# The last expert taken out of the loops of a mixture-of-experts stage, with the next stage's first tiles split meanwhile and the row-pair sums made on VectorE

## What is computed

```python
def moe_ffn(h, router_w, router_b, w_gate_up, b_gate_up, w_down, b_down):
    logits = xt @ router_w + router_b
    top_v, top_i = lax.top_k(logits, TOP_K)            # TOP_K = 4
    gates = jax.nn.softmax(top_v, axis=-1)
    # for every expert e, over the tokens that chose it:
    gu = xb @ w_gate_up[e] + b_gate_up[e]
    act = x_glu * jax.nn.sigmoid(1.702 * x_glu) * (x_lin + 1.0)   # x_glu, x_lin clipped at 7
    out = act @ w_down[e] + b_down[e]                  # times its gate, added to the token's row
x = x + gate2 * rms_norm(moe_ffn(...), g_post_ffn)     # first block ends
x = layer_norm(ALPHA * x + 0.5 * (silu(x @ w1) * (x @ w3)) @ w2, g, b)   # second begins: f1
```

## Time and profile before

| | |
|---|---|
| median of 3 runs | 2604.8 us (2599.99, 2604.8, 2607.95) |
| span of the profiled execution | 2602.5 us |
| TensorE busy | 2430.7 us (93%) |
| VectorE, ScalarE, GpSimd busy | 1115.6, 824.6, 146.0 us |
| granted TensorE clock, mean of the span | 0.99 |
| experts | about 250 to 1233 us of the span |
| f1's first product | 1256.03 us |

### The profile page before, as it was taken

One profiled execution on the slowest core, in us unless ns is written; L12 is line 12 of the kernel. 1 busy time (PEld: TensorE's weight loads), 2 busy tenths in 40 slices (PEclk: granted clock), 3 DMA queues, 4 the chain that ended last, 5 costly groups with the idle time before them and its releaser, 6 DMA issues.

```text
span 2602.5 us, 31931 instructions
## 1 busy us (share of the span) xinstructions
PE 2430.7 (93%) x10874; PEld 1503.4 (58%) x10874; DVE 1115.6 (43%) x1605; ACT 824.6 (32%) x1227; POOL 146.0 (6%) x210
## 2 busy tenths in 40 slices
PE   8999999999988888888999998999999999999999
PEld 4756333333322222222688776777887887777787
DVE  4566111010111111111555677756556556876554
ACT  2322211111111111111444345343444444345443
POOL 0001100010100010000000000000000000100000
PEclk9999999999999999999999999999999999999999
DMA  8768999999999999998556552445555555434554
GB/s 311 270 211 312 411 420 419 421 405 413 406 421 421 421 416 411 407 411 354 174 185 205 168 165 97 162 146 170 186 187 173 188 185 194 150 105 162 170 185 146
DMA packets 263342, 700.36 MB, mean 269 GB/s; under 512 B 29379, under 2 KB 128107, under 8 KB 213536
## 3 DMA queue, kind: packets, MB, share of 16 engines
q1 hardware_dynamic: 249780, 685.19, 71.1%
q0 software_dynamic: 9360, 8.37, 1.0%
q10 hardware_dynamic: 4124, 5.77, 0.6%
HBM read 706.05 MB, written 23.63 MB: 280 GB/s over the span
## 4 chain that ended last, share of the span: by engine, by line
PE 41%; DVE 6%; ACT 2%; issue 2%; DMA 1%; POOL 0%; SPq 0%; POOLq 0%; DVEq 0%; ACTq 0%
PE bank L709 10%; PE bank L711 9%; PE bank L710 9%; PE bank L1313 3%; PE bank L1312 3%; PE bank L1311 3%; PE bank L859 1%; PE bank L801 1%; DVE w_lo L1456 1%; PE bank L1301 1%; PE bank L883 1%; PE bank L783 1%; DVE X L1712 0%; POOL st_out L2826 0%; DVE HTl L1507 0%
## 5 line engine op out<-in xcount | busy, mean ns | idle before, releaser
L1456 DVE TENSOR_TENSOR w_lo<-raw,w_hi 128x1024 fp32r<-128x1024 f32 (+3 forms) x405 | 488.7, 1216 | 342.4 <-ACT w_hi L2464 338.2
L2464 ACT ACTIVATE w_hi<-raw 128x1024 fp32r<-128x1024 f32 (+3 forms) x405 | 426.1, 1057 | 480.3 <-PE bank L711 281.1
L709 PE MATMUL bank<-w_hi,HTh 128*128 128x512 f32 (+1 forms) x1288 | 513.3, 399 | 13.2 <-DVE HTl L1507 8.0
L711 PE MATMUL bank<-w_hi,HTl 128*128 128x512 f32 (+1 forms) x1288 | 503.1, 391 | 0.0
L710 PE MATMUL bank<-w_lo,HTh 128*128 128x512 f32 (+1 forms) x1288 | 502.9, 390 | 0.0
L709 PEld LDWEIGHTS bank<-w_hi,HTh 128*128 128x128 f32 x1288 | 244.3, 190 | 66.5 <-DVE HTl L1507 12.5
L1159 PE MATMUL bank<-W_F,HT_F 128*64 128x512 f32 (+1 forms) x512 | 248.8, 603 | 34.9 <-DMA W_F<-in_moe_w 34.9
L2144 DVE TENSOR_SCALAR arena<-bank 64x512 f32<-64x512 f32 (+1 forms) x64 | 44.3, 693 | 548.9 <-PE bank L1160 548.9
L711 PEld LDWEIGHTS bank<-w_hi,HTl 128*128 128x128 f32 x1288 | 244.3, 190 | 51.9
L710 PEld LDWEIGHTS bank<-w_lo,HTh 128*128 128x128 f32 x1288 | 244.9, 190 | 46.7
L1160 PE MATMUL bank<-W_F,HT_F 128*64 128x512 f32 (+1 forms) x512 | 248.9, 603 | 0.0
(11 more groups left out here) (439 smaller groups left out, 3401.8 us busy)
## 6 DMA issues: line engine op xcount, KB each, us to landing
W_F<-in_moe_w SPq DMA_DIRECT2D x128, 1024.0 KB, 27.2
raw<-in_moe_w SPq DMA_DIRECT2D x64, 1024.0 KB
arena<-in_moe_w SPq DMA_DIRECT2D x64, 1024.0 KB, 26.9
raw<-in_ffn_w SPq DMA_DIRECT2D x248, 256.0 KB, 2.9
raw<-in_ffn_w_gu SPq DMA_DIRECT2D x164, 256.0 KB, 3.0
raw<-in_w_in SPq DMA_DIRECT2D x76, 512.0 KB, 4.8
MIX<-in_moe_w SPq DMA_DIRECT2D x32, 1024.0 KB, 25.1
HT_F<-in_moe_w SPq DMA_DIRECT2D x32, 1024.0 KB
```

Of the source, the lines that this page charges most:

```text
L709: pe.matmul(acc, xh, wh, start=start, stop=False)
L711: return pe.matmul(acc, xl, wh, start=False, stop=stop)
L1456: dve.tensor_tensor(lo_at(n, c), raw_at(n, c), hi_at(n, c).bitcast(F32), ALU.subtract).then_inc(lo_done, 1)
L2464: act.activation(hi_at(n, c), raw_at(n, c), ACT.Copy).then_inc(hi_done, 1)
```

## The change

The loops end one item earlier: `n_items` becomes `n_last`, one less, and the last item is written out behind them on TensorE, VectorE and ScalarE, with other work put between its steps:

- SyncE issues f1's first four tiles directly behind the last expert's weights, each waiting until the slot in `raw` is used (about the sixth tile), and only then waits for the last scatter and issues the row pairs. These go to other places in five copies: MIX (rows 0 and 1 of the first half, 1 MB), XE (row 2, 0.5 MB), AFT_F32 (row 3, 0.5 MB), arena (rows 0 and 1 of the second half), BROWS (rows 2 and 3).
- TensorE leaves out the following item's turning, has the products of `b_down` for both token halves inside the last expert (`down_bias`, into banks 2 to 5), and ends with four products with `LAST_PICK`. The diagonal matrices and their products are gone.
- VectorE makes the sums of both halves (`pair_sum(0)`, `pair_sum(1)`), between steps of the last expert, and adds the banks (`last_rows_added`). The gain is multiplied in while the root is computed.
- ScalarE splits f1's tiles between the steps of the last expert.
- f1's banks are cleared ahead of the transposes of X.

The counters (`taken`, `MOST_ITEMS`, `N_ROOM`) follow; GpSimd's loop ends one item earlier, so one gather fewer is made, and the scatter of the item before the last is written behind it. The diff, its core:

```diff
+        PAIR_LOADS = [(0, 2, MIX), (2, 1, XE), (3, 1, AFT_F32), (4, 2, arena_at(0, 2 * D)), (6, 2, BROWS_OF[:, :])]
+        SUM0, SUM1 = PAIR_ROWS[0], PAIR_ROWS[TOP_K]
...
                 up(1)
-                turn_rows_in(following, 0)
-                if following < P:
-                    turn_rows_in(following, 1)
+                if last:
+                    pe.wait_ge(E("b_down"), 16)
+                    down_bias(it, 0)
+                else:
+                    turn_rows_in(following, 0)
+                    if following < P:
+                        turn_rows_in(following, 1)
                 pe.wait_ge(m_down_read, it * 2 + 2)
                 down(0)
                 turn_act(1)
+                if last:
+                    down_bias(it, 1)
...
-            with pe.Fori(n_runs * (RUN + 1) + 1, n_items) as it:
+            with pe.Fori(n_runs * (RUN + 1) + 1, n_last) as it:
                 expert(it, FEW, FEW)
-            pe.wait_ge(E("b_down"), 16)
+            expert(n_last, FEW, None, last=True)
+            pe.wait_ge(E("last_pick"), 1)
+            pe.wait_ge(m_down_read, n_last * 2 + 4)
             for tt in range(TT):
                 for n in range(2):
...
-                if tt:
-                    for j in range(TOP_K):
-                        pe.wait_ge(E(f"piece_in{2 * tt + j // 2}"), 32)
-                        for n in range(2):
-                            a = D * (j % 2) + 512 * n
-                            mm = pe.matmul(last_sum(tt, n), DIAG[:, j, :], moe_slot(PAIRS_IN[2 + j // 2])[:, a:a + 512], start=False,
-                                           stop=(j == TOP_K - 1))
+                    mm = pe.matmul(last_sum(tt, n), LAST_PICK[:, tt, :], OUTE[:, 512 * n:512 * (n + 1)], start=False, stop=True)
                 mm.then_inc(E("moe_over"), 1)
...
+            def pair_sum(tt):
+
+                for j in range(TOP_K):
+                    dve.wait_ge(E(f"piece_in{PAIR_LANDED[TOP_K * tt + j]}"), 32)
+                    o, g, to = PAIR_ROWS[TOP_K * tt + j], GATE_P[:, tt, j:j + 1], (SUM0, SUM1)[tt]
+                    if j == 0:
+                        step(dve.tensor_scalar(to, o, g, None, ALU.mult))
+                    else:
+                        step(dve.scalar_tensor_tensor(to, o, g, to, ALU.mult, ALU.add))
...
+            take_linear(last, 0, FEW)
+            activate(last, 0, FEW)
+            pair_sum(0)
+            take_linear(last, 1, FEW)
+            activate(last, 1, FEW)
+            split_to(n1 + 1)
+            pair_sum(1)
+            split_to(n1 + 2)
+            out_half(last, FEW)
+            split_to(n1 + 3)
+            last_rows_added(0)
+            signal("moe_sum")
+            step(dve.tensor_tensor(PAIR_ROWS[1], SUM0, gate2, ALU.mult))
             k = rsqrt(stat(), 1.0 / D, 1e-6)
+            last_rows_added(1)
+            step(dve.scalar_tensor_tensor(X[:, 0, :], PAIR_ROWS[1], rooted(k), X[:, 0, :], ALU.mult, ALU.add))
             signal("x1")
+            step(dve.tensor_tensor(PAIR_ROWS[TOP_K + 1], SUM1, gate2, ALU.mult))
+            k = rsqrt(stat(), 1.0 / D, 1e-6)
             rows_half(0)
+            split_to(n1 + 4)
+            step(dve.scalar_tensor_tensor(X[:, 1, :], PAIR_ROWS[TOP_K + 1], rooted(k), X[:, 1, :], ALU.mult, ALU.add))
             signal("x1")
...
+            take_glu(last, 0, FEW)
+            gated(last, 0, FEW)
+            act_taken(last, 0, FEW)
+            act.wait_ge(m_used, moe_used(last, 9))
+            split_to(n1 + 2)
+            take_glu(last, 1, FEW)
+            gated(last, 1, FEW)
+            split_to(n1 + 3)
+            act_taken(last, 1, FEW)
+            split_to(n1 + 4)
+            out_half(last, FEW)
+            for s in (SUM0, SUM1):
+                row_sum(s, ACT.Square)
...
+                    load_ffn(FFN["f1"], True, lambda i: sp.wait_ge(m_used, n_last * MOE_TILES + MOE_TILES + 4 + (FFN["f1"].n0 + i) % RAW // 2 * 2))
+                    sp.wait_ge(m_out, n_last * 16 + 16)
                     sp.sem_inc(E("rows_over"), 1)
...
+                    for i, (a, n, place) in enumerate(PAIR_LOADS):
+                        tt, j = a // TOP_K, a % TOP_K
+                        if i == 1:
+                            sp.wait_ge(m_gather, n_last * 2 + 2)
+                            sp.wait_ge(m_rows, n_last * 16 + 16)
+                        if j == 0:
+                            sp.wait_ge(m_used, n_last * MOE_TILES + MOE_TILES + (2, 12)[tt])
+                        src = pair_dram.ap()[P * TOP_K * tt:P * TOP_K * (tt + 1), :].rearrange("(p j) n -> p (j n)", j=TOP_K)
+                        dst = place if len(place.shape) == 2 else place[:, :, :].rearrange("p a b -> p (a b)")
+                        sp.dma_start(dst, src[:, D * j:D * (j + n)]).then_inc(E(f"piece_in{i}"), 16)
```

More of the change, by code:

```diff
@@ L1131, in _, with expert @@
             pe.wait_ge(E("moe_bias_landed"), 32)
-            def expert(it, many, following, between=None):
+            def expert(it, many, following, between=None, last=False):
                 low, high = slice(0, many), slice(P - many, P)
@@ L1151, in up @@
                             turn_act(0)
-                        if t == 15:
+                        if t == 15 and not last:
                             pe.wait_ge(m_rows, it * 16 + 16)
@@ L1206, in expert, with last_sum, down_bias @@
                 down(1)
+            def last_sum(tt, n):
+                return bank[2 + 2 * tt + n][:, :]
+            def down_bias(it, tt):
+                pe.wait_ge(m_glu_read, it * 2 + tt + 3)
+                pe.wait_ge(m_lin_read, it * 2 + tt + 3)
+                for n in range(2):
+                    pe.matmul(last_sum(tt, n), GATET[:, tt * P:(tt + 1) * P], BDOWN[:, 512 * n:512 * (n + 1)], start=True, stop=False)
             expert(0, FEW, FEW, routing_between)
@@ L1266, in ffn @@
                         if tt == 0 and i == 2:
-                            if name != "f3":
+                            if name not in ("f1", "f3"):
                                 clear_banks()
@@ L2172, in _, with last_rows_added @@
                 expert(run * (RUN + 1) + (RUN + 1), CAP, FEW)
-            with dve.Fori(n_runs * (RUN + 1) + 1, n_items) as it:
+            with dve.Fori(n_runs * (RUN + 1) + 1, n_last) as it:
                 expert(it, FEW, FEW)
+            def pair_sum(tt):
[6 more added lines that the diff above has]
+                        step(dve.scalar_tensor_tensor(to, o, g, to, ALU.mult, ALU.add))
+            def last_rows_added(tt):
+                dve.wait_ge(E("moe_over"), tt + 1)
+                s = (SUM0, SUM1)[tt]
+                for n in range(2):
+                    c = slice(512 * n, 512 * (n + 1))
+                    ins = dve.tensor_tensor(s[:, c], s[:, c], bank[2 + 2 * tt + n][:, :], ALU.add)
+                step(ins)
+                ask(tt)
+            last, n1 = n_last, FFN["f1"].n0
             dve.wait_ge(E("last_rows"), 2)
@@ L2193, in _ @@
-            dve.wait_ge(E("moe_over"), 1)
-            for n in range(2):
-                c = slice(512 * n, 512 * (n + 1))
-                ins = dve.tensor_tensor(SUM0[:, c], SUM0[:, c], bank[2 + n][:, :], ALU.add)
-            step(ins)
-            for i in range(1 + TT):
-                ask(i)
-            split_to(FFN["f1"].n0 + 2)
+            take_linear(last, 0, FEW)
[3 more added lines that the diff above has]
+            activate(last, 1, FEW)
```

96 lines of the change are left out of this document (25 added, 71 removed).

## The result

The changed kernel takes 2615.24 us (median of 13 runs, 2607.67 to 2621.6) against 2604.8 us (median of 13, 2598.51 to 2609.05): a ratio of 1.0044, 95% interval 1.0033 to 1.0054, slower by 8.6 to 14.1 us. The profiled execution has a span of 2616.7 us, 14.2 over that of before. Of the runs further down, one of root_first (3479.61 us) and one of before beside it (8499.53 us) were far slower than all others and are left out.

A forecast was written before the change was run, and what follows sets the result against it. Weight copies bound the experts; the change touches the seam before f1, the third feed-forward. Waiting for pair copies, the expert's rest, the sum and f1's start put f1's second transposes 8.3 us later: median 2613.1, range 2603 to 2619.

The forecast's parts named there:

- Copies: SyncE's queue at the seam: f1's 2 MB land by 1236.5, then the pairs, from MIX 1239.1 to BROWS 1246.9.
- The new wait: VectorE's `pair_sum(0)` waits for AFT_F32 (1241.7) ahead of the second half's clip; TensorE stands from 1227.9 to 1244.5.
- Rest of the expert: TensorE's remaining last-expert work after the wait: 6.8 us at full clock plus 2.5 for the lower clock, to 1253.8.
- The sum: From the last down product through pick products, adding, root and X to f1's first product: 1253.8 to 1265.2.
- f1's start: TensorE's first twelve f1 products, then the second transposes at 1269.5 against 1261.19: 8.3 us later.
- Sum: Whole kernel: +8.3 us, bounds from the clock +6.6 to +10.0; profiled 2610.8, median 2613.1.
- B: Rival: pair copies land in time, AFT_F32 by about 1222, so the clip doesn't wait; 2593.7 us; chance 0.17.
- C: Rival: lag of the slow DMA engines half as long, landings 4 to 12 us earlier, about 2604.8; chance 0.09.
- D: Rival: the copy line is slower, f1's 2 MB taking 8 us in place of 5.2; 2616 us; chance 0.06.

The follow-up runs named there:

- root_first: Kernel before the change, with ScalarE's square sum ahead of its splits of f1's tiles and VectorE's root and X's first half ahead of its own: ratio 0.9968.
- vector_order: Changed kernel with the second half's clip and product ahead of `pair_sum(0)` on VectorE, ScalarE's order kept: 1.0030 against the kernel before.
- pairs_first: Changed kernel with the last expert's steps ahead of sums and splits, pairs issued ahead of f1's tiles, VectorE's root and X ahead of its splits: 1.0000 against before.
- other_queue: Changed kernel with the five pair copies issued on ScalarE's queue and ScalarE's splits of f1's tiles behind `out_half`: 2623.92 us, single run.
- clock_filled: Changed kernel with 19 unused float32 products on TensorE ahead of its wait in the last expert's `down(0)`: 1.0046 against the kernel before.
- tiles_first_only: Kernel before the change, with only f1's first four tiles issued ahead of the row pairs: ratio 0.9995.

## Why the prediction was right, point by point

The forecast was 2613.1 in a range of 2603 to 2619; 2615.2 was measured, and the branch was the likeliest one. By its own steps, times of after less 1.0 for the axis in brackets:

- *Copies.* This step held. Landings forecast: MIX 1239.1, XE (Y in the rows) 1240.4, AFT_F32 (AFT_F) 1241.7, arena 1244.3, BROWS 1246.9. Measured, issue and landing time added: 1240.2, 1241.8, 1243.1, 1245.6 and 1248.0 (1239.2, 1240.8, 1242.1, 1244.6, 1247.0). All within 0.4. One sentence on them was wrong all the same: the pairs were not "in line before the laggards are done with PRPT", since the issue of f1's tiles held SyncE until 1232.0. It made no difference to the landings: a copy came by what was ahead of it, whether it waited in the queue or SyncE waited to issue it. The row of before that hinted at it is PRPT's issue of 4.34 us, where MIX's took 0.33. The 9.74 us beneath are no such sign: the two issues in that row took 0.32 each, and between them SyncE waited until TensorE had used the second slot (1228.3).
- *The new wait.* Clip forecast at about 1243, measured 1245.1 (1244.1). The bound was mis-chosen: I let AFT_F32's landing set it, but VectorE's four operations behind MIX do (0.75 and three of 1.32 from 1240.28, to 1245.0). TensorE idle 17.7 instead of 16.6. "ScalarE's new wait costs nothing more" held only because VectorE's lay over it: alone it is worth 9.26 (vector_order).
- *Rest of the expert.* This is the term that was mis-sized. Forecast 9.3 us from the resumption to the end of the last down product, 6.8 and 2.5 for the clock; measured 12.7. I had the clock come back 3 to 7 us after the work resumed. The down products' spacing shows it coming back between 1258.1 and 1258.8, 11.4 to 12.1 us after: 0.85 apart at 1257.23 to 1258.08, then 0.70, and 0.43 before the wait. So all but the last products of the expert ran at 1.2 GHz, and cost 5.9 us over 6.8, not 2.5. The 3 to 7 us had been read behind an idle stretch of 5.54 us and carried over to one three times as long; no row of before showed what such a stretch does.
- *The sum.* Forecast 11.4 us from the last down product to f1's first, measured 10.8. GpSimd's power for the root took 0.58 us where the row of before gave 1.49; that moved the bound to the adding of the second half, 0.15 us ahead of X, and of the 0.9 us only 0.3 were left (1.50 from st_in to X for the 1.77 forecast). Another 0.4 lie between X and f1's product: these transposes took 1.24 us where before's took 1.97. `pair_sum(1)` and the splits were over at 1253.65, 5.7 ahead of the end of the last down product: hidden, as said.
- *f1's start.* Forecast 4.3 to the second transposes, measured 5.3: the twelve products ran 0.43 apart all through, which is the bound that the prediction gave for the lower clock.
- *Sum.* Forecast +8.3. The profile has +13.2 from U. Above the forecast are 1.1 of idle time, 3.4 in the rest of the expert and 1.0 in f1's start, below it 0.6 in the sum; the medians have +10.4, and their interval (8.6 to 14.1) begins just above my figure. The terms were short by 4.9, of which 4.4 are TensorE's clock. That the forecast still lies within 2.1 us of the time measured is in part luck: the medians moved 2.8 less than the profile did.
- *Rivals.* B (copies in time) would have shown the clip at 1223; it stood at 1245. C and D asked for landings 4 to 12 us earlier or 3 later than forecast; they were within 0.4. B's price, 11.4 us from the last down product to f1's first with the copies in time, stays untested. pairs_first, where no copy is waited for, has 18.5, with 7.08 of TensorE standing for VectorE's sums, but both sums stand behind `out_half` there. B has one of them ahead of the clip and the other beside the down products, where VectorE stood idle 7.73 us before the clip and 7.90 before `out_half`; that was not run. The fit of the Trainium skill that the paragraph on B uses (DMA: Bandwidth & Descriptors, Anatomy of one DMA) is given there for a copy that GpSimd issues; MIX is issued by SyncE, so its 20.9 us are no test of the fit itself.
- *Not in the working.* The steps took 11.3 us off the stretch behind the last down product (22.7 to 11.4), and 12.0 were measured. But the kernel before lost 5 us there for another reason, the mean square behind the splits. The prediction read that row (1247.92) and used it only to say that early copies by themselves gain nothing; root_first shows that a reordering without any of the change takes these 5 us (22.8 to 17.4).

## What to carry to other kernels

Before an engine is given a wait for a copy, look at what stands behind the wait in its program, and at who else waits in the same stretch: here two engines each put one wait ahead of work that TensorE needed, and removing one only uncovered the other. Take the time of a landing from the copies in line in front of it, not from its issue or its size, and put what needs no copy (the expert's own steps, the mean square) ahead of what does: for the mean square alone that made this kernel about 0.3% faster. And when a sum is moved from an idle stretch of one engine to another engine, count it as work on the path until a row shows that it is hidden.

## What the runs showed of the hardware

- Eight copies of 256 KB took SyncE 20.56 us to issue (20.52 to 20.60 in four more kernels), though the last products to read the slots that they fill ended at 1211.43. It was the issue itself that stood still, and with it what was behind it on SyncE: the second copy of each tile has no wait of its own, and in after these issues took 3.40, 4.56, 1.07 and 1.79 us. The form of the copy alone doesn't do it: before, the same eight, issued when the weights had landed, took 0.43 to 0.96 us each and once 4.26. The five pair copies behind them took 0.33 to 0.78 each. In other_queue, with ScalarE's copies in the same engines, the eight took 30.05 us. Tiles and pairs landed in the order of SyncE's program, however early the waits of a copy were over.
- After an idle stretch of 17.7 us TensorE worked for 11.4 to 12.1 us without a pause in its rows before its clock went from 1.2 to 2.4 GHz, and after 9.26 us of idle time in vector_order for 10.5 to 11.3; in clock_filled it fell while the rows show it busy. The Trainium skill (TensorE: Matmul & The Clock Gate, What's actually happening) gives the two levels, the lower for an idle and the full for a busy engine; the rows after the idle stretch and the fall in clock_filled don't fit that, and a term for the clock should be bounded by the whole of the work behind the idle stretch.
- The same power of 128x1 on GpSimd took 1.49 us or 0.55 to 0.58, by what VectorE did beside it:

```profile
1249.33 1.49 POOL L2826 TENSOR_TENSOR st_out<-st_in,TAB 128x1 f32<-128x1 f32 x1 [22.88 <-DVE st_in L1547]
1265.40 0.58 POOL L2840 TENSOR_TENSOR st_out<-st_in,TAB 128x1 f32<-128x1 f32 x1 [58.45 <-DVE st_in L1550]
```

The first is of before, the second of after. Before, VectorE was subtracting for a tile of f1 from 1249.15 to 1250.37 (`w_lo<-raw,w_hi`, no bank among its operands), and the power ended 0.44 us behind it; tiles_first_only has the same subtraction beside it and 1.48 us. At the seam of the other seven kernels, after included, VectorE either ran an operation that reads a bank or none as the power began, and it took 0.58. No run changed this alone, so it is a pattern of nine traces; but a root on the path is better not given a split of VectorE to run beside.
